# A one-core encoder layer: sums of the queries' squares from rounded high and low parts, and another lag in the key stage

## The chip, the cores and the metric

The kernel runs on one core of one Trainium2 chip. The metric is the device time of one execution in microseconds (us), lower is better. A difference of about 0.2% is what a measurement of this kernel can tell from no change.

## What is computed

One layer of a streaming encoder, for 1024 prompt tokens and 32 sample tokens (T = 1056 in all), width 1024, everything in fp32. The part that the change touches is the normalisation of queries and keys per head, before the attention:

```
xn = rms_norm(x, attn_norm)
z = xn @ w_in
q, k, v, xl, yg, gl = jnp.split(z, IN_SPLITS, axis=-1)
q = partial_rope(rms_norm(q.reshape(B, T, N_HEADS, HEAD_DIM), q_norm), positions)
k = partial_rope(rms_norm(k.reshape(B, T, N_KV_HEADS, HEAD_DIM), k_norm), positions)
...
y = x32 * lax.rsqrt(jnp.mean(x32 * x32, axis=-1, keepdims=True) + RMS_EPS)     # rms_norm
```

There are 16 query heads and 4 key heads of 64. A query sees the keys of its own chunk of 64 tokens and the chunk before. Around it stand an RG-LRU branch, output projections and a SwiGLU.

## The kernel before

Features lie on the 128 partitions, tokens in the free dimension. A dense product of this part takes one 128x1024 unit of weights and makes three blocks of 352 tokens. Each fp32 operand is split into a rounded high part and a low part (`wh`, `wl`, `acth`, `actl`, all of type f32r), and a block is 8 chunks times 3 products (high x high, high x low, low x high), so 24 matmuls. POOL makes the two parts of the next unit of weights (`split`, L522 and L524, two halves each, into a slot of two) once PE has ended the unit that was in that slot.

The program is written out by hand for each engine; the order on an engine is the order in the code, and semaphores tie the engines together. The stages that matter here are these.

- **The values**: nine products; ACT copies each from its bank to `vst` (L1054) and stores it by DMA, with two buffers. At the end ACT issues four more stores.
- **The key stage**: PE makes six blocks of keys (`qk(late, keys=True)`, 2 units x 3 blocks), then six of the first group's queries. For each block ACT runs `qk_copy`: one pass into `qsb` with the gain (L1074) and one that squares the bank. For keys the squares go into `qsq` (L1077), and PE sums them over each head with one unsplit fp32 product against `heads` (`k_sums`), which is issued two blocks late. ACT takes the root into `qstd` (`k_root`, L1087), also two copies late. DVE (`rope_k`) makes the rotation with three instructions (`halves`, L1505 to L1507), adds (L1513), takes the reciprocal of `qstd` (L1515) and multiplies (L1520).
- **The query stage**, four times, once for each group g: six blocks; ACT writes `qsb` (L1074) and the squares (L1081). The squares of group g lie in `ot[g % 2]`, the buffer which the attention of that group fills later. DVE (`rope_q`) makes `halves` and one addition into `qt` (L1525). The scale of the queries isn't multiplied in: it enters later, in the attention's `Exp`.
- **A group** (`group(g)`): PE runs four units of gate products (`dense`, 288 matmuls), and after each of them `each()` counts. After the 18th, `q_sums` issues one product for each of the 17 chunks of tokens: 128 columns of squares as the stationary operand against two columns of `heads`, unsplit fp32. After the 66th, the first attention step is issued, and one more after each 11. ACT takes the root of these sums (`q_root`, L1094), DVE the reciprocal (`q_inverse`, L1532).

The sixth block's place is the end of the query stage: on ACT and DVE its copies and its rotation run while PE is already in the first gate unit of the group.

Of the kernel before, what the change touches and what calls it, by code (L numbers as in the profile page):

```python
# [260 lines left out]
def build(nc, small_in, x_in, cs_in, w_in, kc_in, vc_in, y_out, kp_out, vp_out, ks_out, vs_out, tail_out):  # L261
# [21 lines left out]
    with ctx:  # L283
# [50 lines left out]
        with ExitStack() as s:  # L334
            cs = tensor(s, "cs", [P, 2, T])
            qsb = tensor(s, "qsb", [P, 2, BW])
            qsq = tensor(s, "qsq", [P, 2, BW])
            pt = tensor(s, "pt", [P, 2, 2 * P])
            kg = tensor(s, "kg", [P, 2, KW])
            vgr = tensor(s, "vgr", [P, AU, HD])  # L340
            qt = tensor(s, "qt", [P, 2 * T])
            tg = tensor(s, "tg", [P, 3, BW])
            pr = tensor(s, "pr", [P, 3, 2, P])
            ot = tensor(s, "ot", [P, 2, 2, T])
            snk = tensor(s, "snk", [P, 2, 2])
            sm = tensor(s, "sm", [P, 3, 6, 2])
            qroot = tensor(s, "qroot", [P, AU, 2])
            qinv = tensor(s, "qinv", [P, 2, AU, 2])
        early.close()
# [29 lines left out]

        def qsquares(g):  # L380

            return ot[:, g % 2, :, :].rearrange("p i t -> p (i t)")

# [52 lines left out]
        def flat(a):  # L436
# [21 lines left out]
            sem("rope_sin"), sem("rope_cos"), sem("rope_sum"), sem("k_rstd"), sem("rope_done"))  # L458
        heads_done, gains_loaded = sem("head_columns"), sem("gains_loaded")
        qss_done, qroot_done, qinv_done = sem("q_sumsq"), sem("q_root"), sem("q_inverse")  # L460
        k_stored = [sem(f"k_stored{i}") for i in range(2)]
# [131 lines left out]
        def _(pe):  # L593
# [131 lines left out]
            def qk(late, keys=False):  # L725

                for i in range(2):
                    for n in range(NB):
                        job = dense_block(i, n, acth, actl)
                        if keys:  # L730
                            late.append((NB * i + n, job.bank, job.after))
                        if late and (not keys or NB * i + n >= 2):
                            k_sums(*late.pop(0))
                return job

            def q_sums(g, job):

                wait(pe, free[job.bank], job.after)
                wait(pe, std_done, 6)
                wait(pe, qroot_done, 2 * g)  # L740
                wait(pe, ot_done, AU * g)
                for u in range(AU):
                    q, _, q0 = unit_shape(u)
                    i = mm(aux0[0:2 * q, 2 * u:2 * u + 2], qsquares(g)[:, 2 * q0:2 * (q0 + q)], heads[:, 0:HD:HD // 2],
                           start=True, stop=True)
                i.then_inc(qss_done, 1)
# [46 lines left out]
            def group(g, late):  # L793
                done = [0, 0]

                def each():
                    done[0] += 1
                    if done[0] == 18:
                        q_sums(g, late)
                    if done[1] < ASLOTS and done[0] == step_mm(done[1]):  # L800
# [122 lines left out]
        def _(act):  # L923
# [136 lines left out]

            act.wait_ge(unit_done, plan.units.value())
            act.wait_ge(v_stored[0], 16 * 5)
            act.wait_ge(v_stored[1], 16 * 4)
            act.wait_ge(stored, 16 * 3)
            act.wait_ge(gains_loaded, 32)


            def qk_copy(base, k, gain):
# [9 lines left out]
                else:  # L1078
                    g = base // 6 - 1
                    wait(act, ot_stored[g % 2], 16 * (g // 2))  # L1080
                    f(by_unit(qsquares(g), k % NB, k // NB), ps.rearrange("p (b t) -> p b t", t=HT), ACT.Square)\  # L1081
                        .then_inc(free[job.bank], 1)

# [5 lines left out]
            def q_root(g):  # L1089

                for j, (rows, units) in enumerate(((slice(0, P), slice(0, AU - 1)), (slice(0, 2 * DEC), slice(AU - 1, AU)))):
                    wait(act, qss_done, g + 1)
                    wait(act, qinv_done, 4 * g)
                    f(qroot[rows, units, :], aux0[rows, 2 * units.start:2 * units.stop].rearrange("p (u h) -> p u h", h=2),  # L1094
                      ACT.Sqrt, scale=1.0, bias=HD * EPS).then_inc(qroot_done, 1)
# [16 lines left out]
            qgain, kgain = gains[:, 0:1], gains[:, 1:2]  # L1112
            for j in range(12):
                qk_copy(j // 6 * 6, j % 6, (kgain, qgain)[j // 6])
                if 2 <= j < 8:
                    k_root(j - 2)
                if 3 <= j < 9:
# [213 lines left out]
        def _(dve):  # L1331
# [190 lines left out]
            def rope_q(base, k):  # L1522

                halves(base, k)
                V.tensor_tensor(by_unit(qt, k % NB, k // NB), rt1[:, :].rearrange("p (b t) -> p b t", t=HT),  # L1525
                                rt2[:, :].rearrange("p (b t) -> p b t", t=HT), ALU.add).then_inc(rope_done, 1)

            def q_inverse(g):
# [10 lines left out]
            for j in range(4):  # L1539
                rows = slice(j * HD // 2, (j + 1) * HD // 2)  # L1540
                V.memset(heads[rows, :].rearrange("p (s h n) -> p h s n", s=2, h=2)[:, j % 2], 1.0).then_inc(heads_done, 1)
            V.memset(kg[:, :, :], 0.0).then_inc(kz_done, 1)
            dve.wait_ge(cs_loaded, 32)
# [662 lines left out]
```

## Time and profile before

| | |
|---|---|
| median of three runs | 1673.92 us (1672.77 to 1674.69) |
| the profiled execution | 1678.89 us |
| its span | 1677.0 us |
| PE busy | 1620.6 us, 97% of the span |
| PE weight load busy | 1540.2 us |
| DVE, ACT, POOL busy | 1006.5, 626.0, 942.3 us |

PE is the engine that has nearly no idle time, so what counts is where PE stands still, what it issues that isn't a dense product, and which clock it is granted (TensorE has two levels, 1.2 and 2.4 GHz, given as 0.50 and 1.00). The other engines count where PE waits for them.

### The profile page before, as it was taken

How to read it: one execution, taken by the hardware profiler on the slowest of the kernel's cores; microseconds unless marked ns; L12 is line 12 of the kernel's file. 1: busy time of each engine (PE TensorE's matmuls, PEld its weight loads, DVE VectorE, ACT ScalarE, POOL GpSimd, SP SyncE). 2: the span in 40 equal slices, each digit the busy share in tenths (PEclk: the TensorE clock that was granted, in tenths of full speed). 3: DMA queues.
4: the chain of work that ended last, by engine and by line, in shares of the span. 5: the costliest groups of instructions: out<-in, count | busy, mean ns of one | idle time of the engine just before them, and what ended most of it. 6: DMA issues, size and time to landing. Idle time of an engine off the chain costs nothing. (4 is left out here: it accounts for less than half of the span.)

```text
span 1677.0 us, 28467 instructions
## 1 busy us (share of the span) xinstructions
PE 1620.6 (97%) x11270; PEld 1540.2 (92%) x11270; DVE 1006.5 (60%) x1718; ACT 626.0 (37%) x1294; POOL 942.3 (56%) x685
## 2 busy tenths in 40 slices
PE   7999998899999999999898999999999999999999
PEld 4899998889989898898897989999999999998998
DVE  6677555855545546757888878333333334869585
ACT  5535551243342525524224334333333333433232
POOL 4545542212313121468775718777677677786876
PEclk9999999999999999999999999999999999999999
DMA  5111122313132140364343512222242222373643
GB/s 183 45 51 64 63 79 84 89 56 113 47 105 67 56 128 31 101 251 165 118 154 103 180 52 79 81 83 78 77 179 78 77 77 77 141 275 117 246 143 147
DMA packets 73032, 182.09 MB, mean 109 GB/s; under 512 B 15092, under 2 KB 26676, under 8 KB 72260
## 3 DMA queue, kind: packets, MB, share of 16 engines
q1 hardware_dynamic: 52228, 160.35, 27.3%
q10 hardware_dynamic: 20672, 19.93, 3.8%
q8 instruction: 90, 1.47, 0.4%
q14 instruction: 42, 0.34, 0.1%
HBM read 131.23 MB, written 49.28 MB: 108 GB/s over the span
## 5 line engine op out<-in xcount | busy, mean ns | idle before, releaser
L597 PE MATMUL bank<-xh,wsh 128*128 128x264 f32 x2170 | 623.3, 287 | 21.8 <-POOL wsl L573 7.6
L597 PE MATMUL bank<-xh,wsl 128*128 128x264 f32 x2170 | 619.7, 286 | 0.0
L597 PE MATMUL bank<-xl,wsh 128*128 128x264 f32 x2170 | 618.8, 285 | 0.0
L597 PEld LDWEIGHTS bank<-xh,wsh 128*128 128x128 f32 x2170 | 411.3, 190 | 25.5 <-issue 16.6
L597 PEld LDWEIGHTS bank<-xl,wsh 128*128 128x128 f32 x2170 | 411.3, 190 | 0.2
L597 PEld LDWEIGHTS bank<-xh,wsl 128*128 128x128 f32 x2170 | 411.2, 190 | 0.0
L597 PE MATMUL bank<-acth,wh 128*128 128x352 f32 x960 | 318.6, 332 | 5.5 <-POOL wl L524 3.6
L597 PE MATMUL bank<-acth,wl 128*128 128x352 f32 x960 | 314.7, 328 | 0.0
L597 PE MATMUL bank<-actl,wh 128*128 128x352 f32 x960 | 313.4, 326 | 0.0
L522 POOL TENSOR_SCALAR wh<-wraw 128x512 fp32r<-128x512 f32 (+1 forms) x100 | 73.2, 732 | 404.6 <-PE bank L597 382.2
L573 POOL TENSOR_TENSOR wsl<-praw,wsh 128x512 fp32r<-128x512 f32 (+1 forms) x157 | 245.9, 1566 | 84.6 <-ACT wsh L1211 84.5
L573 POOL TENSOR_TENSOR wsl<-wsum,wsh 128x512 fp32r<-128x512 f32 (+1 forms) x120 | 185.3, 1544 | 82.5 <-ACT wsh L1211 82.4
L1211 ACT ACTIVATE wsh<-praw 128x512 fp32r<-128x512 f32 (+1 forms) x157 | 97.2, 621 | 261.7 <-PE bank L597 234.6
L597 PEld LDWEIGHTS bank<-acth,wh 128*128 128x128 f32 x960 | 183.3, 191 | 9.2 <-POOL actl L529 2.7
L597 PEld LDWEIGHTS bank<-actl,wh 128*128 128x128 f32 x960 | 183.7, 191 | 0.6
L597 PEld LDWEIGHTS bank<-acth,wl 128*128 128x128 f32 x960 | 183.0, 191 | 0.4
L1800 DVE TENSOR_TENSOR ev<-bank,ev 128x264 f32<-128x264 f32 x126 | 53.8, 431 | 158.9 <-PE bank L597 158.9
L524 POOL TENSOR_TENSOR wl<-wraw,wh 128x512 fp32r<-128x512 f32 (+1 forms) x100 | 143.4, 1434 | 8.4
L1211 ACT ACTIVATE wsh<-wsum 128x512 fp32r<-128x512 f32 (+1 forms) x120 | 74.2, 619 | 195.1 <-POOL wsum L569 120.3
L1607 DVE TENSOR_TENSOR xl<-acc,xh 128x2112 fp32r<-128x2112 f32 (+1 forms) x47 | 131.8, 2805 | 22.4 <-ACT xh L1228 22.4
L1704 DVE SCALAR_TENSOR_TENSOR ev<-bank,ev 128x264 f32<-128x264 f32 x90 | 38.7, 430 | 138.2 <-PE bank L597 137.6
L569 POOL TENSOR_TENSOR wsum<-praw,wsum 128x512 f32<-128x512 f32 (+1 forms) x45 | 71.5, 1589 | 80.7 <-PE bank L597 80.7
(179 smaller groups left out, 2305.6 us busy)
## 6 DMA issues: line engine op xcount, KB each, us to landing
praw<-in_weights SPq DMA_DIRECT2D x34, 1024.0 KB, 5.0
wraw<-in_weights SPq DMA_DIRECT2D x52, 512.0 KB, 3.3
h_scratch<-ev SPq DMA_DIRECT2D x44, 264.0 KB, 2.0
acc<-h_scratch SPq DMA_DIRECT2D x4, 2112.0 KB, 12.7
ev<-x_scratch SPq DMA_DIRECT2D x6, 1056.0 KB, 5.0
spare<-x_scratch SPq DMA_DIRECT2D x6, 1056.0 KB, 4.9
praw<-in_weights SPq DMA_DIRECT2D x8, 768.0 KB, 5.1
ta_scratch<-tg ACTq DMA_DIRECT2D x24, 176.0 KB, 1.9
```

Of the source, the lines that this page charges most:

```text
L522: nc.gpsimd.tensor_scalar(high, raw, 1.0, 0.0, ALU.mult, ALU.add).then_inc(split_done, 1)
L524: nc.gpsimd.tensor_tensor(low, raw, high.bitcast(f32), ALU.subtract).then_inc(split_done, 1)
L569: nc.gpsimd.tensor_tensor(dst, a, b, op).then_inc(wsum_done, 1)
L573: nc.gpsimd.tensor_tensor(w_slot(wsl, p, r), w_part(p, r), w_slot(wsh, p, r).bitcast(f32), ALU.subtract)\
L597: return nc.tensor.matmul(*args, **kw)
L1211: f(w_slot(wsh, p, r), w_part(p, r), ACT.Copy).then_inc(whi_done, 1)
L1607: V.tensor_tensor(xl[k][:, 0:n, :], x_part(t, k), xh[k][:, 0:n, :].bitcast(f32), ALU.subtract)\
L1704: stt(u2(par, n), bank[BANKS[2][n]][:, 0:QB], scale, u2(par, n), ALU.mult, ALU.add).then_inc(u2_done, 1)
L1800: V.tensor_tensor(dst, bank[BANKS[r][n]][:, 0:QB], (u4(par, n), None, u2(par, n), u2(par, n))[r - 3], ALU.add).then_inc(done, 1)
```

## The change

- `k_sums` and `k_root` are issued one block after the block they belong to, not two. Before the first copy of the key stage ACT no longer waits for the landing of the value stores and for the end of the value units; that wait stands before the first query copy (j == 6).
- The queries' squares are no longer summed in fp32. ACT squares the bank into `qsq`, rounds that into a high part (f32r, one more pass over `qsplit`), and DVE subtracts it from the squares to give a low part (one more pass after each `rope_q`). `q_sums` issues two accumulating f32r products for each of the 17 chunks, 34 in all, against `marks`, an f32r copy of the two columns of `heads`; the last chunk takes 128 columns too. They are issued after the 24th gate matmul instead of the 18th, and they wait for the low part of the sixth block (`qlow_done`).
- `qsplit` lies in the memory of `ot`: the high part of group g in half g % 2, the low part in the other half, which for g > 0 waits until the attention output of group g - 1 has been stored from it.

```diff
@@ tensors
+            with ExitStack() as squares:
+                qsplit = tensor(squares, "qsplit", [P, 2, 2 * T], f32r)
             ot = tensor(s, "ot", [P, 2, 2, T])
+            marks = tensor(s, "marks", [P, 2], f32r)
@@ PE
-                        if late and (not keys or NB * i + n >= 2):
+                        if len(late) > keys:
                             k_sums(*late.pop(0))
-                wait(pe, free[job.bank], job.after)
+                wait(pe, qlow_done, 6 * g + 6)
                 wait(pe, std_done, 6)
+                wait(pe, marks_done, 1)
                 wait(pe, qroot_done, 2 * g)
                 wait(pe, ot_done, AU * g)
                 for u in range(AU):
-                    q, _, q0 = unit_shape(u)
-                    i = mm(aux0[0:2 * q, 2 * u:2 * u + 2], qsquares(g)[:, 2 * q0:2 * (q0 + q)], heads[:, 0:HD:HD // 2],
-                           start=True, stop=True)
+                    c0 = min(u * P, 2 * T - P)
+                    for low in range(2):
+                        i = mm(aux0[:, 2 * u:2 * u + 2], qsquares(g, low)[:, c0:c0 + P], marks[:, :],
+                               start=low == 0, stop=low == 1)
...
-                    if done[0] == 18:
-                        q_sums(g, late)
+                    if done[0] == 24:
+                        q_sums(g)
@@ ACT
-            act.wait_ge(unit_done, plan.units.value())
-            act.wait_ge(v_stored[0], 16 * 5)
-            act.wait_ge(v_stored[1], 16 * 4)
-            act.wait_ge(stored, 16 * 3)
+            act.wait_ge(unit_done, 2 * V_PAIR)
...
-                    g = base // 6 - 1
+                    g, j = base // 6 - 1, base - 6 + k
+                    wait(act, ss_done, min(5 + j, 6))
+                    wait(act, qlow_done, j - 1)
+                    f(qsq[:, k % 2, :], ps, ACT.Square).then_inc(free[job.bank], 1)
                     wait(act, ot_stored[g % 2], 16 * (g // 2))
-                    f(by_unit(qsquares(g), k % NB, k // NB), ps.rearrange("p (b t) -> p b t", t=HT), ACT.Square)\
-                        .then_inc(free[job.bank], 1)
+                    wait(act, free[job.bank], job.after)
+                    f(by_unit(qsquares(g), k % NB, k // NB), qsq[:, k % 2, :].rearrange("p (b t) -> p b t", t=HT), ACT.Copy)\
+                        .then_inc(qhigh_done, 1)
...
             for j in range(12):
+                if j == 6:
+                    act.wait_ge(v_stored[0], 16 * 5)
+                    act.wait_ge(v_stored[1], 16 * 4)
+                    act.wait_ge(stored, 16 * 3)
                 qk_copy(j // 6 * 6, j % 6, (kgain, qgain)[j // 6])
-                if 2 <= j < 8:
-                    k_root(j - 2)
+                if 1 <= j < 7:
+                    k_root(j - 1)
@@ DVE, at the end of rope_q
+                g, j = base // 6 - 1, base - 6 + k
+                dve.wait_ge(qhigh_done, j + 1)
+                if g:
+                    dve.wait_ge(ot_stored[(g + 1) % 2], 16 * ((g + 1) // 2))
+                V.tensor_tensor(by_unit(qsquares(g, 1), k % NB, k // NB), qsq[:, k % 2, :].rearrange("p (b t) -> p b t", t=HT),
+                                by_unit(qsquares(g), k % NB, k // NB).bitcast(f32), ALU.subtract).then_inc(qlow_done, 1)
```

On ACT, at the start of the key stage (`qsb` and `qsq` of each block of keys, `qstd` its root), before:

```order
L1074 ACTIVATE qsb<-bank,gains 128x352 [waits outputs_stored,gains_loaded,v_stored1,job_done,v_stored0,unit_done]
L1077 ACTIVATE qsq<-bank 128x352
L1074 ACTIVATE qsb<-bank,gains 128x352 [waits job_done]
L1077 ACTIVATE qsq<-bank 128x352
L1074 ACTIVATE qsb<-bank,gains 128x352 [waits rope_cos,unit_done]
L1077 ACTIVATE qsq<-bank 128x352 [waits k_sumsq]
L1087 ACTIVATE qstd<-bank 128x352 [waits k_sumsq]
```

and after:

```order
L1077 ACTIVATE qsb<-bank,gains 128x352 [waits job_done,gains_loaded,unit_done]
L1080 ACTIVATE qsq<-bank 128x352
L1077 ACTIVATE qsb<-bank,gains 128x352 [waits job_done]
L1080 ACTIVATE qsq<-bank 128x352
L1094 ACTIVATE qstd<-bank 128x352 [waits k_sumsq]
L1077 ACTIVATE qsb<-bank,gains 128x352 [waits rope_cos,unit_done]
L1080 ACTIVATE qsq<-bank 128x352 [waits k_sumsq]
```

The three waits for stores have left the first row, and the root of the first block stands after the second copy instead of the third.

On DVE, two blocks of the query stage of group 0 (`rt` the rotation, `qt` its sum), before:

```order
L1505 SCALAR_TENSOR_TENSOR rt<-qsb,cs 64x352 [waits rope_done,qk_copied]
L1506 SCALAR_TENSOR_TENSOR rt<-qsb,cs 64x352
L1507 TENSOR_TENSOR rt<-qsb,cs 128x352
L1525 TENSOR_TENSOR qt<-rt 128x11x32 [waits rope_cos,rope_sin]
L1505 SCALAR_TENSOR_TENSOR rt<-qsb,cs 64x352 [waits rope_done,qk_copied]
```

and after:

```order
L1517 SCALAR_TENSOR_TENSOR rt<-qsb,cs 64x352 [waits rope_done,qk_copied]
L1518 SCALAR_TENSOR_TENSOR rt<-qsb,cs 64x352
L1519 TENSOR_TENSOR rt<-qsb,cs 128x352
L1537 TENSOR_TENSOR qt<-rt 128x11x32 [waits rope_cos,rope_sin]
L1543 TENSOR_TENSOR qsplit<-qsq,qsplit 128x11x32 [waits q_squares_high]
L1517 SCALAR_TENSOR_TENSOR rt<-qsb,cs 64x352 [waits rope_done,qk_copied]
```

A fifth instruction, with two operands in SBUF, stands between one block's rotation and the next one's.

On PE, in the first gate unit of group 0, the products that sum the queries' squares, before:

```order
L597 MATMUL bank<-acth,wl 128x352
L597 MATMUL bank<-heads,ot 128x2 [waits k_std,bank_free2]
L597 MATMUL bank<-heads,ot 128x2 x15
L597 MATMUL bank<-heads,ot 64x2
L597 MATMUL bank<-acth,wh 128x352
```

and after:

```order
L601 MATMUL bank<-acth,wl 128x352
L601 MATMUL bank<-marks,qsplit 128x2 [waits head_marks,k_std,q_squares_low]
L601 MATMUL bank<-marks,qsplit 128x2 x33
L601 MATMUL bank<-acth,wh 128x352 [waits bank_free1]
```

17 instructions become 34, and the wait for ACT's last square (`bank_free2`) becomes one for DVE's last low part.

## Rows read from the trace of the kernel before

**Rows 1.** The page's busy time: us (share of the span), instructions of each engine.

```profile
PE 1620.6 (97%) x11270; PEld 1540.2 (92%) x11270; DVE 1006.5 (60%) x1718; ACT 626.0 (37%) x1294; POOL 942.3 (56%) x685
```

**Rows 2.** Waits of PE from 255 to 342 us: engine line <- releaser: us, times, longest.

```profile
PE bank L597 <- ACT qstd L1087: 5.9, 4, 1.9
PE bank L597 <- ACT qsq L1077: 2.5, 1, 2.5
```

**Rows 3.** Timeline of ACT, start of the key stage: start us, us, instruction [idle before <-releaser].

```profile
276.53 0.55 ACT L1074 ACTIVATE qsb<-bank,gains 128x352 f32<-128x352 f32 x1 [3.26 <-DMA out_tail<-tail]
```

**Rows 4.** Timeline of DVE in the key stage, one key block and the next one's start.

```profile
284.58 0.52 DVE L1505 SCALAR_TENSOR_TENSOR rt<-qsb,cs 64x352 f32<-64x352 f32 x1
...
287.60 2.35 DVE L1515 RECIPROCAL qstd<-qstd 128x352 f32<-128x352 f32 x1 [0.76 <-ACT qstd L1087]
...
290.69 0.52 DVE L1505 SCALAR_TENSOR_TENSOR rt<-qsb,cs 64x352 f32<-64x352 f32 x1
```

**Rows 5.** Who waited for tile qstd, 270 to 320 us.

```profile
  DVE qstd L1515: 4.3, 6
  DVE rt L1505: 0.5, 1
```

**Rows 6.** Timeline of DVE and POOL, end of group 0's query stage.

```profile
322.87 0.62 POOL L522 TENSOR_SCALAR wh<-wraw 128x512 fp32r<-128x512 f32 x1 [7.49 <-PE bank L597]
...
323.89 1.51 DVE L1506 SCALAR_TENSOR_TENSOR rt<-qsb,cs 64x352 f32<-64x352 f32 x1
...
331.95 0.53 DVE L1525 TENSOR_TENSOR qt<-rt 128x352 f32<-128x352 f32 x1
```

**Rows 7.** Timeline of PE, two dense matmuls 24 apart, group 0's last query block.

```profile
318.22 0.32 PE L597 MATMUL bank<-acth,wh 128*128 128x352 f32 x1
...
322.07 0.32 PE L597 MATMUL bank<-acth,wh 128*128 128x352 f32 x1
```

**Rows 8.** Timeline of PE: the queries' sums and the first attention step, groups 0, 1, 3.

```profile
327.31 4.46 PE L597 MATMUL bank<-heads,ot 128*128 128x2 f32 x34 [1.72 <-ACT ot L1081]
...
341.98 0.38 PE L597 MATMUL bank<-kg,qt 128*128 128x128 f32 x2
423.41 0.72 PE L597 MATMUL bank<-heads,ot 128*128 128x2 f32 x6
...
438.03 0.38 PE L597 MATMUL bank<-kg,qt 128*128 128x128 f32 x2
615.53 0.39 PE L597 MATMUL bank<-heads,ot 128*128 128x2 f32 x3
...
628.61 0.38 PE L597 MATMUL bank<-kg,qt 128*128 128x128 f32 x2
```

**Rows 9.** Windows, PE: us, busy (x) of PE, PEld, DVE, ACT, POOL, granted clock, DMA.

```profile
330.40:337.30 6.90, 6.90 (x27) 6.87 (x27) 2.67 (x10) 2.00 (x4) 0.00 (x0) 0.51 0.75 130
426.00:432.80 6.80, 6.80 (x28) 6.77 (x28) 1.54 (x7) 1.99 (x4) 0.39 (x1) 0.50 0.21 77
620.60:624.00 3.40, 3.40 (x14) 3.40 (x13) 0.00 (x0) 0.81 (x2) 0.00 (x0) 0.50 0.81 274
```

**Rows 10.** Windows of the sums' products alone: PE, PEld, DVE, granted clock, DMA.

```profile
423.40:426.00 2.60, 2.59 (x24) 2.60 (x25) 0.00 (x0) 1.00 0.00 0
426.10:427.70 1.60, 1.60 (x9) 1.60 (x8) 0.00 (x0) 0.50 0.17 31
```

**Rows 11.** Timeline of DVE at group 1's and group 3's sums.

```profile
419.69 2.35 DVE L1641 TENSOR_TENSOR acc<-acc 128x2112 f32<-128x2112 f32 x1
...
425.37 1.40 DVE L1525 TENSOR_TENSOR qt<-rt 128x352 f32<-128x352 f32 x1
...
616.48 1.40 DVE L1525 TENSOR_TENSOR qt<-rt 128x352 f32<-128x352 f32 x1
```

**Rows 12.** Weight loads, mean ns: groups by line, f32r (acth) and fp32 (heads, qsq).

```profile
L597 PEld LDWEIGHTS bank<-acth,wl 128*128 128x128 f32 x960 | 183.0, 191 | 0.4
...
L597 PEld LDWEIGHTS bank<-qsq,heads x12: 186/187/190, 277.5 to 306.5; 128*128 128x128 f32 x12
```

More of the change, by code:

```diff
@@ L378, in build, with qsquares @@
         fifth = spare[:, :].rearrange("p (c t) -> p c t", t=HALF)
-        def qsquares(g):
-            return ot[:, g % 2, :, :].rearrange("p i t -> p (i t)")
+        def qsquares(g, low=0):
+            return qsplit[:, (g + low) % 2, :]
         def by_unit(a, n, i):
@@ L459, in build @@
         heads_done, gains_loaded = sem("head_columns"), sem("gains_loaded")
+        marks_done, qhigh_done, qlow_done = sem("head_marks"), sem("q_squares_high"), sem("q_squares_low")
         qss_done, qroot_done, qinv_done = sem("q_sumsq"), sem("q_root"), sem("q_inverse")
@@ L731, in qk, with q_sums @@
                             late.append((NB * i + n, job.bank, job.after))
-                        if late and (not keys or NB * i + n >= 2):
+                        if len(late) > keys:
                             k_sums(*late.pop(0))
                 return job
-            def q_sums(g, job):
-                wait(pe, free[job.bank], job.after)
+            def q_sums(g):
+                wait(pe, qlow_done, 6 * g + 6)
                 wait(pe, std_done, 6)
+                wait(pe, marks_done, 1)
                 wait(pe, qroot_done, 2 * g)
@@ L1089, in q_root @@
             def q_root(g):
-                for j, (rows, units) in enumerate(((slice(0, P), slice(0, AU - 1)), (slice(0, 2 * DEC), slice(AU - 1, AU)))):
+                for rows, bank_rows, units in ((slice(0, P), slice(0, P), slice(0, AU - 1)),
+                                               (slice(0, 2 * DEC), slice(P - 2 * DEC, P), slice(AU - 1, AU))):
                     wait(act, qss_done, g + 1)
                     wait(act, qinv_done, 4 * g)
-                    f(qroot[rows, units, :], aux0[rows, 2 * units.start:2 * units.stop].rearrange("p (u h) -> p u h", h=2),
+                    f(qroot[rows, units, :], aux0[bank_rows, 2 * units.start:2 * units.stop].rearrange("p (u h) -> p u h", h=2),
                       ACT.Sqrt, scale=1.0, bias=HD * EPS).then_inc(qroot_done, 1)
@@ L1541, in _ @@
                 V.memset(heads[rows, :].rearrange("p (s h n) -> p h s n", s=2, h=2)[:, j % 2], 1.0).then_inc(heads_done, 1)
+            dve.wait_ge(heads_done, 5)
+            V.tensor_copy(marks[:, :], heads[:, 0:HD:HD // 2]).then_inc(marks_done, 1)
             V.memset(kg[:, :, :], 0.0).then_inc(kz_done, 1)
```

## The prediction

> **What bounds the kernel now.** I read the busy time first, then the waits of PE, then the timeline of each engine around the one product that the change replaces, and the granted clock there.
>
> PE is busy for 97% of the span [rows 1]. Every time that PE stands still or runs at half clock is therefore time of the kernel, unless it stood still there anyhow; what DVE and ACT do costs only where PE waits for it. Two places matter.
>
> In the key stage PE waits for ACT's copies and roots, 5.9 and 2.5 us, 8.4 in all [rows 2]. ACT in turn waits for DVE, which is the slow engine there: a key block takes it 290.69 - 284.58 = 6.1 us, of which 0.76 is a wait for the root [rows 4], 4.3 us over six blocks, and 0.5 us more behind the last [rows 5]. A block of PE takes 322.07 - 318.22 = 3.85 us, so 0.16 us a matmul [rows 7]. So DVE leaves the key stage with a backlog: it ends the sixth query block of group 0 at 332.5 us [rows 6], while PE started the queries' sums at 327.3 [rows 8]. Before, that backlog cost PE only 1.72 us, since the sums needed ACT's squares and nothing of DVE.
>
> At the queries' sums themselves PE makes products of two columns. Their records (two for each of the 17 fp32 products) come 2.60 / 24 = 0.11 us apart, and at half clock 1.60 / 9 = about 0.2 [rows 10], so 3.8 us for all. Behind them the clock falls to 0.50 for 6.8 us in group 0 and 1 and for 3.4 in group 3 [rows 9]; group 2 is like group 1. The whole price per group is read from the distance between the first of these products and the first attention step: 48 dense matmuls are 7.7 us of it, the rest is sums and lost clock. Group 0: 14.67 - 7.7 = 7.0. Group 1: 14.62 - 7.7 = 6.9; group 2 the same. Group 3: 13.08 - 7.7 = 5.4 [rows 8].
>
> **The change part by part.**
>
> The products. 34 f32r products take the place of 34 fp32 records. No row shows an f32r product over two columns, but what sets the pace of the old ones is the load of 128 stationary columns, and such a load has the same length in both types, 191 ns for f32r and 187 for fp32 [rows 12]. I take 0.11 us each, so 3.8 us as before; the last chunk's 128 columns for 64 add 0.1. Bounds: half of it (1.9 us), if a load in f32r is shorter than its record lets one see, and twice (7.6 us), if each instruction makes two records as an fp32 one does. The Trainium skill speaks against my value: its page "TensorE: Matmul & The Clock Gate", section "Weight-path perf modes — Fast Weight Load (FWL) and DoubleRow", says that a load of 128 columns in a type other than FP32 takes a faster path, about twice as fast as measured on trn2. If f32r counts as such a type, each group saves about 1.9 us by that rule; the equal records of [rows 12] speak against it.
>
> The key stage. Two things make DVE earlier. The first copy no longer waits for stores: before, it came 3.26 us after the work ahead of it [rows 3], most of that DMA issue on ACT's own queue up to 275.2, so the gain is 276.5 - 275.2 = 1.3 us. And the root comes before DVE asks for it, since sum and root each stand a block earlier: the 4.3 + 0.5 us of waits go [rows 5]. PE now waits longer for the first sum (after two blocks, not three) but hardly afterwards, and I walk it to the end of the query blocks at 319, some 3 us earlier than 322. That gain is spent at once, as follows.
>
> The low parts. DVE gets 24 more instructions of two SBUF operands, like L1525, which take 0.53 us [rows 6] plus 0.1 between instructions; ACT gets 24 more passes of about 0.5 us, beside PE's 3.85 us a block, which hide. In group 0 nothing hides DVE's: it works through its backlog without a pause. Its end moves from 332.5 by -1.3 - 4.8 + 6 x 0.63 to 330.2. But a two-operand instruction of DVE slows while POOL splits a weight unit, 1.51 us for 0.52 [rows 6]. Such a split follows each of PE's units, four times in this stage, for 4.4 us each; before, most fell on reciprocals or on waits. With the waits gone I count 3 us more, so 333.4, between 330.2 (the collisions of before) and 335.
>
> Group 0. PE comes to the new sums at 319 + 24 x 0.16 = 322.9 and waits until 333.4, ten us. After such a wait I expect half clock: 34 x 0.215 = 7.3 us, to 340.7 (a little under twice the pace at full clock, and near the 0.2 of [rows 10]). Then the remaining 42 dense matmuls (6.7 us), with 2.6 us lost as the clock stays at half for about the 5 us that it did before. First attention step at 350.0 for 341.98 [rows 8]: **+8.0**. Bounds: DVE's end at 330.2 and full clock in the sums gives +1.3; 335 gives +9.6.
>
> Groups 1 to 3. Here DVE keeps up (four instructions and the fifth are 3 us a block, for 3.85), but the last block counts. In group 3 its rotation collides with the split and ends at 616.48 + 1.40 = 617.9 [rows 11]; the low part follows until 618.5. PE reached the old place at 615.53 and the new one, six matmuls later, at 616.5. So it waits 2.1 us where it waited for nothing. Group 2 is the same. In group 1 a 2.35 us sum for a later stage stands ahead of the sixth block on DVE, whose rotation ends at 426.8 [rows 11]; with the low parts of the fifth and sixth block I get 428.0, PE is there at 424.4, and waits 3.6 us. The idle time lies directly before 3.8 us of products of two columns, which already pull the clock down, so part of these now runs at half clock (0.1 us more for each of 34, at most 3.5) and the fall can last another stretch (3.4 us, so 1.7 lost). Bounds for the clock: 0 and 5.2 us a group. I take 2.5 in group 1, 1.5 in group 2, and 3 in group 3, which had only the short fall before. **+6.1, +3.6, +5.1**.
>
> Edits that cost nothing by cover: `marks` (one copy on DVE, before the keys arrive), the later issue of the sums (42 dense matmuls, 6.7 us, still cover ACT's root and DVE's inverse, some 2.5 us; without this cover PE would wait for them at the first step), the wait for the stored attention output (issued at 398.7 in group 1, landed some 5 us later, and the first low part is due at 404.6; a landing 3 us later would show on DVE, which has 0.8 us a block to make up for it).
>
> Sum: 8.0 + 6.1 + 3.6 + 5.1 = 22.8 us on the profiled span of 1677.0; everything behind group 3's sums is bound by PE and moves along. The profiled execution took 1678.9, 5 us over the median of the runs shown, and the difference of the two kernels should not hang on that. So 1673.9 + 22 = **1696 us**. With all lower bounds (1.3 + 3.6 + 2.1 + 2.1) it is 1683, with all upper ones (9.6 + 8.8 + 7.3 + 7.3) 1707.
>
> **The rivals.**
>
> *The clock takes no notice.* The waits cost their own time and nothing more. For it: in group 3 the sums alone cost only one short stretch. Against: every stretch of these products is followed by half clock [rows 9]. Time: 4.7 in group 0, 7.8 in the others, 1686.
>
> *The f32r products are short.* 1.9 us a group instead of 3.8, 3.6 for 7.3 at half clock. For it: each makes one pass of its moving side. Against: rows 12. That alone saves 3.7 + 3 x 2 or so: 1682 to 1687.
>
> *The f32r products are short and keep the clock up, the one that ends on the other side.* Place: the sums of each group. Price: after the wait, 1.9 us and no fall, in place of 6.9, 6.9 and 5.4: group 1 3.6 + 1.9 - 6.9 = -1.4, group 2 -2.9, group 3 -1.4, group 0 still some +3. Sum -2.7, 1671. It decides the sign from the point at which wait and products together take less than the 6.9 us of before. Against it: what pulls the clock down seems to be products of two columns, and they stay.
>
> *Each f32r product makes two records.* 3.8 us more in each of four groups, up to twice that at half clock: 1711 to 1720. For it: fp32 does so; against: f32r products over 256 and 352 columns make one.
>
> *The change doesn't do what it says*: the low part of the last block might land before PE comes there. In groups 2 and 3 that needs DVE 2 us earlier, while the split that slows it starts with the same event as the block. I see no way, 2%.
>
> **How the numbers follow.** Forecast with its own bounds (slower, 1687 to 1705): 0.62. Clock takes no notice: 0.12. Short products: 0.10. Short and clock up: 0.07, split between faster and same. Two records: 0.07. Last one: 0.02, same. The range of 8 in 10 takes in the forecast, the first two rivals and the upper bound: 1680 to 1706. Within 0.2% is 1670.6 to 1677.3, about what a measurement of this kernel can tell from no change; faster 0.04, same 0.06, slower 0.90.
>
> **What would show it.** In the profile after: no wait of DVE for `qstd`; the sums of group 0 starting at 331 to 335, with PE idle for about ten us ahead of them, ended by DVE's `qsplit`; 34 records at about 0.11 us (0.21 where the clock is 0.50); idle times of 3.6, 2.1 and 2.1 us in groups 1 to 3; first attention steps at about 350, 452, 552 and 651. Fewer or longer records than these, or a clock of 1.00 behind the sums, would move the sum as in the rivals. An idle time of under 5 us in group 0 would mean that my count of DVE's chain is wrong.

## The result, and the profile after

| | before | after |
|---|---|---|
| median | 1674.26 us (1672.77 to 1674.69, 4 runs) | 1693.62 us (1692.02 to 1696.4, 4 runs) |
| ratio | 1 | 1.0113, 95% interval 1.0101 to 1.0125 |
| the profiled execution, its span | 1678.89, 1677.0 us | 1692.57, 1690.8 us |

The change makes the kernel 1.1% slower, 19.4 us by the medians. The forecast was 1696 us. The profiled execution of before isn't one of its four runs and lies 4.6 us above their median, so the two profiles are only 13.7 us apart.

The waits of PE, from 255 to 350 us (group 0) and from 350 to 660 us (the other three), in the kernel after; they answer to [rows 2]:

```profile
PE bank L601 <- DVE qsplit L1543: 7.1, 1, 7.1
PE bank L601 <- ACT qsq L1085: 1.6, 1, 1.6
PE bank L601 <- ACT qsq L1080: 1.4, 1, 1.4
...
PE bank L601 <- DVE qsplit L1543: 6.7, 3, 3.2
PE bank L601 <- DVE ot L1606: 1.2, 3, 0.4
```

The waits for `qstd` have gone. In their place PE waits for the low parts that DVE makes: 7.1 us in group 0 and 6.7 in the three other groups. PE's timeline, the sums and the first attention steps, answers to [rows 8]:

```profile
327.62 0.59 PE L601 MATMUL bank<-marks,qsplit 128*128 128x2 f32 x2 [7.09 <-DVE qsplit L1543]
...
327.86 7.18 PE L601 MATMUL bank<-marks,qsplit 128*128 128x2 f32 x33
343.09 0.38 PE L601 MATMUL bank<-kg,qt 128*128 128x128 f32 x2
...
428.83 0.38 PE L601 MATMUL bank<-marks,qsplit 128*128 128x2 f32 x2 [3.19 <-DVE qsplit L1543]
...
444.20 0.27 PE L601 MATMUL bank<-kg,qt 128*128 128x128 f32 x1
...
628.17 0.38 PE L601 MATMUL bank<-marks,qsplit 128*128 128x2 f32 x2 [1.73 <-DVE qsplit L1543]
...
641.93 0.27 PE L601 MATMUL bank<-kg,qt 128*128 128x128 f32 x1
```

The sixth block's last instructions on DVE in group 3 (to be read beside [rows 11]) show why 1.73 us are waited there: a split of POOL runs from 622.8 to 627.3, the rotation's last instruction takes 1.41 us beside it instead of 0.53, and the low part stands behind it.

```profile
626.27 1.41 DVE L1537 TENSOR_TENSOR qt<-rt 128x352 f32<-128x352 f32 x1
627.60 0.51 DVE L1543 TENSOR_TENSOR qsplit<-qsq,qsplit 128x352 fp32r<-128x352 f32 x1
```

And the windows at half clock (us, busy (x) of PE, PEld, DVE, ACT, POOL, granted clock, DMA share, GB/s), which answer to [rows 9]:

```profile
324.30:338.00 13.70, 10.38 (x45) 10.38 (x46) 3.84 (x13) 2.11 (x4) 0.00 (x0) 0.50 0.34 73
430.10:440.30 10.20, 10.20 (x43) 10.20 (x43) 0.61 (x4) 2.11 (x4) 0.00 (x0) 0.50 0.05 20
529.10:539.30 10.20, 10.20 (x44) 10.20 (x45) 0.61 (x4) 2.11 (x4) 0.00 (x0) 0.50 0.11 43
631.50:638.30 6.80, 6.80 (x26) 6.80 (x26) 0.61 (x4) 2.11 (x4) 0.00 (x0) 0.50 0.28 99
```

Each stretch is 3.4 or 6.9 us longer than before: 41.0 us at half clock between 300 and 700 us for 23.9 (6.8 + 6.8 + 6.8 + 3.4); in group 0, PE stands still for 3.3 us of its stretch. From one group's first step to the next, after takes 101.1, 99.7 and 98.0 us, where before took 96.1, 96.1 and 94.5 (its group 2 steps at 534.11 us, the others are in [rows 8]). That is 12.2 us for the groups 1 to 3, of which 6.7 are idle time and the rest goes with the clock. Behind the last of these steps the two profiles are alike: 1690.8 - 641.93 = 1048.9 us and 1677.0 - 628.61 = 1048.4. Only group 0 looks nearly unchanged, 343.1 for 342.0. The experiments explain that.

### The profile page after: what moved, and what is told of

Same layout as the page of the kernel before. It is cut to its first block and busy times, and to the rows that moved or that the text cites. A ratio compares the mean times of both kernels' runs of the same rounds, so it can differ in the third digit from the quotient of the medians.

```text
span 1690.8 us, 28567 instructions
## 1 busy us (share of the span) xinstructions
PE 1629.9 (96%) x11270; PEld 1550.2 (92%) x11270; DVE 1019.7 (60%) x1743; ACT 638.7 (38%) x1318; POOL 947.2 (56%) x685
## 3 DMA queue, kind: packets, MB, share of 16 engines
q1 hardware_dynamic: 52228, 160.35, 27.3%
## 5 line engine op out<-in xcount | busy, mean ns | idle before, releaser
L601 PE MATMUL bank<-acth,wl 128*128 128x352 f32 x960 | 315.2, 328 | 0.0
L577 POOL TENSOR_TENSOR wsl<-praw,wsh 128x512 fp32r<-128x512 f32 (+1 forms) x157 | 254.2, 1619 | 84.6 <-ACT wsh L1223 84.6
```

The costliest lines, as they stand in the source:

```text
L577: nc.gpsimd.tensor_tensor(w_slot(wsl, p, r), w_part(p, r), w_slot(wsh, p, r).bitcast(f32), ALU.subtract)\
L601: return nc.tensor.matmul(*args, **kw)
```

## The experiments

My theory: after is slower because DVE's low parts make PE wait, and the wait lengthens the stretch at half clock; the key stage alone gains. Rivals: f32r products over two columns are dearer (or cheaper) than fp32 ones; the key stage counts for nothing; the clock has nothing to do with the wait. Each group of runs was compared with before on its own chip, whose median was 1675.6 to 1676.9 us, so the ratios are to be compared and not the times. The last column is read from one profiled execution of each kernel.

| kernel | ratio to before, 95% interval | at half clock between 300 and 700 us |
|---|---|---|
| after, once more | 1.0091 (1.0070 to 1.0111) | 41.0 |
| key stage alone | 0.9972 (0.9959 to 0.9984) | 23.9 |
| split sums alone | 1.0126 (1.0113 to 1.0140) | 44.4 |
| after, sums behind the 48th matmul | 1.0005 (0.9992 to 1.0019) | 27.3 |
| after, group 0's sums behind the 60th | 1.0066 (1.0045 to 1.0088) | 30.7 |
| after, high products alone | 1.0015 (1.0003 to 1.0027) | 23.9 |
| after, no low parts | 0.9951 (0.9937 to 0.9965) | 20.5 |
| key stage, fp32 sums behind the 48th | 0.9941 (0.9918 to 0.9964) | 20.5 |
| before, sums spread | 0.9970 (0.9951 to 0.9988) | 20.5 |
| key stage, sums spread | 0.9961 (0.9946 to 0.9976) | 17.1 |
| key stage, sums spread where nothing waits | 0.9904 (0.9888 to 0.9919) | 0.0 |

### Before once more

> The kernel before once more, for a second profile of the same program. In the first profile of before the copies of the key stage began at 276.5 us, in the one of after at 271.6, although only some 1.3 us of that can be the change. Theory: the landing of the value stores differs from execution to execution, so a second profile shows the first key copy somewhere else, by up to 4 us, and the first attention step of group 0 with it. Rival: the start is fixed at 276.5 and the change moved it by 5 us.

Its profiled execution took 1676.22 us. Timeline of ACT at the start of the key stage:

```profile
271.18 0.46 ACTq L1059 DMA_DIRECT2D out_tail<-tail  x1
274.43 0.56 ACT L1074 ACTIVATE qsb<-bank,gains 128x352 f32<-128x352 f32 x1 [4.77 <-DMA out_tail<-tail]
```

The first copy comes at 274.4, not at 276.5 [rows 3]; the copies of `vst` ahead of it wait for landings, and those differ. So the theory holds, and the rival falls: of the 5 us between the two first profiles some 2 are the execution's own. What the prediction didn't have: in this execution the last store was issued at 271.2 and the copy still had to wait for landings that take up to 4 us, so taking the waits away gives 2.9 us here, not 1.3. In the executions with the new key stage the first copy began at 270.6 to 272.2 us, in the four with the old one at 274.4 to 276.5. The first step of group 0 stands at 339.7 here, so after's 343.1 is 3.4 us late against this profile and 1.1 against the first.

### The two parts of the change alone

```diff
-            act.wait_ge(unit_done, plan.units.value())
-            act.wait_ge(v_stored[0], 16 * 5)
...
-                        if late and (not keys or NB * i + n >= 2):
+                        if len(late) > keys:
...
-                if 2 <= j < 8:
-                    k_root(j - 2)
+                if 1 <= j < 7:
+                    k_root(j - 1)
```

> Before with the key stage of after (sums and roots a block earlier, stores waited for later), the queries' sums untouched. Theory: DVE's waits for the roots go (4.8 us in the profile of before) and the first copy comes 1.3 us or more earlier, which lets PE end the query blocks of group 0 earlier: 2 to 5 us faster, 1670 to 1672, nothing changed in groups 1 to 3. Rival: PE's longer wait for the first sum takes it all back, no change at 1674. In the first case the split sums alone cost more than the whole change does.

0.9972: 4.7 us faster, at the upper end of what was expected. PE waits in the stage:

```profile
PE bank L597 <- ACT ot L1078: 2.6, 1, 2.6
PE bank L597 <- ACT qsq L1074: 1.2, 1, 1.2
PE bank L597 <- POOL wh L522: 0.9, 1, 0.9
```

The 5.9 us of waits for `qstd` [rows 2] have gone. 0.9 us of waits for POOL are new: PE comes so early that the next unit's split isn't ready.

The second half, after with these edits undone:

> After with the key stage of before. Theory: the low parts' work comes on top of the whole backlog of DVE: idle time before group 0's sums of about 10 us instead of 7.1 + 1.6, and 3.2, 1.7, 1.7 us in groups 1 to 3 as in after: 1697 to 1700. Rival: the key stage counts for nothing in either kernel, then 1694 as after.

1.0126, 21 us slower than before and 1696.9 in its own chip's times. The theory's sign is right, the size at its lower end (1697 to 1700). The idle time ahead of group 0's sums didn't grow to 10 us: PE's waits for `qstd` came back, 6.4 us, and beside them stand the same 7.0 us for the low part.

```profile
PE bank L601 <- DVE qsplit L1542: 7.0, 1, 7.0
PE bank L601 <- ACT qstd L1097: 6.4, 4, 2.0
```

That follows from the chains: the old key stage makes DVE late and PE late as well, by about the same amount. The parts add up within their intervals: -0.28% and +1.26% make +0.98% beside the +1.13% and +0.91% of the two comparisons of after.

### The wait taken away by covering it

```diff
-                    if done[0] == 24:
+                    if done[0] == 48:
                         q_sums(g)
```

> After with the queries' sums issued after the 48th gate matmul instead of the 24th, 3.85 us of dense work later. Theory (PE waits for the last low part, and the wait lengthens the stretch at half clock): the idle times of groups 1 to 3 (3.2, 1.7, 1.7) go, group 0's 7.1 falls to 3.3, so 10.5 us less idle time, and 4 to 6 us less lost to the clock: 1678 to 1682. Rival (the products themselves or their number cost the time, the wait is beside it): 1690 or more, with the stretches of half clock as long as in after.

1.0005: the loss against before has gone, with all low parts made and all 34 products issued. That is 0.9 to 1.1% under after, 14 to 18 us, where the theory had 14 to 17. A part of this is the gain of the key stage, which this kernel has as well: against the key stage alone (0.9972) 0.3% are still lost. The waits of PE from 255 to 660 us:

```profile
PE bank L601 <- DVE qsplit L1543: 3.3, 1, 3.3
PE bank L601 <- DVE ot L1606: 1.6, 4, 0.4
```

The three waits of groups 1 to 3 have gone, group 0's has fallen by the 3.85 us of dense work. In groups 1 to 3 the stretches at half clock are 6.8, 6.8 and 0 us. So the rival that puts the time into the products falls. Group 0, where 3.3 us of the wait are left, keeps its long stretch:

```profile
327.80:341.50 13.70, 13.46 (x56) 13.46 (x57) 0.98 (x8) 2.47 (x5) 0.00 (x0) 0.50 0.20 40
```

```diff
-                    if done[0] == 24:
+                    if done[0] == (24 if g else 60):
```

> After with the sums of group 0 alone issued after the 60th gate matmul; those of groups 1 to 3 stay after the 24th. Theory: group 0's idle time falls from 7.1 to about 1.3 us and the clock isn't low when its sums start: 6 to 9 us below after, of the 17 that the move of all four groups to the 48th brought; groups 1 to 3 keep their idle times of 3.2, 1.7 and 1.7 us and their stretches at half clock. Rival (the groups 1 to 3 hold nearly all): 3 us or less.

1.0066, so 4 us under after on the same chip (1.0091) and 8 under the first comparison; 6 to 9 were expected, and with so wide an interval the times alone don't decide between this and the rival. By the profile group 0's first step comes at 334.9 us, 8.2 before after's, and groups 1 to 3 keep their three waits:

```profile
PE bank L601 <- DVE qsplit L1543: 8.0, 4, 3.2
```

The stretches at half clock, in the order of the groups:

```profile
328.70:338.90 10.20, 10.20 (x41) 10.15 (x42) 1.95 (x9) 3.80 (x11) 1.40 (x2) 0.50 0.11 37
424.20:431.00 6.80, 6.80 (x30) 6.80 (x30) 0.61 (x4) 2.11 (x4) 0.00 (x0) 0.50 0.01 2
523.20:530.00 6.80, 6.80 (x28) 6.80 (x28) 0.61 (x4) 2.11 (x4) 0.00 (x0) 0.50 0.00 0
622.20:629.00 6.80, 6.80 (x26) 6.80 (x26) 0.61 (x4) 2.11 (x4) 0.00 (x0) 0.50 0.25 90
```

Here the expectation was wrong: with the same waits of 3.2, 1.7 and 1.7 us, groups 1 and 2 have 6.8 us at half clock and not 10.2, as much as in the first profile of before, where nothing is waited for. So the wait does not lengthen the stretch by the same amount in every execution. Over groups 1 to 3 the stretches add up to 20.4 us here, to 27.3 in both profiles of after and to 30.7 in the kernel with the split sums alone, against 17.1 in both profiles of before: longer each time, by 3 to 14 us.

Against the key stage alone, whose first step is at 335.96 us and which takes 286.6 us from there to group 3's, after loses 7.1 us in group 0 and 12.3 in the other three. This kernel has nothing of the first loss and 11.0 us of the second. By the profiles group 0 thus holds some four tenths of what the split sums cost.

### What the products cost

```diff
-                    for low in range(2):
-                        i = mm(aux0[:, 2 * u:2 * u + 2], qsquares(g, low)[:, c0:c0 + P], marks[:, :],
-                               start=low == 0, stop=low == 1)
+                    i = mm(aux0[:, 2 * u:2 * u + 2], qsquares(g)[:, c0:c0 + P], marks[:, :], start=True, stop=True)
```

> After with only the 17 products of the high parts: the low part is still made by DVE and waited for, but left out of the sums. Theory: the idle times stay (7.1, 3.2, 1.7, 1.7) and each missing product saves 0.11 us at full and 0.21 us at half clock, so 1.9 to 3.6 us a group, 8 to 14 in all, with some stretches of half clock shorter: 8 to 16 us below after. Rival (a second product into the same sums costs nearly nothing, or the time is all in the wait): within 3 us of after.

1.0015, 13 to 16 us under after, the upper end of the theory, while PE's waits for `qsplit` are the same 13.7 us:

```profile
426.16 2.06 PE L601 MATMUL bank<-marks,qsplit 128*128 128x2 f32 x17 [3.20 <-DVE qsplit L1541]
...
PE bank L601 <- DVE qsplit L1541: 13.7, 4, 7.0
```

The 17 products take 2.06 us and the next matmul begins 1.92 us after their start, so 0.11 each. More than half of the gain is the clock: 23.9 us at half clock for 41.0. In this kernel the waits are there and the stretches add up to what they do in before. So the wait alone doesn't lengthen them; the next kernel shows the same of a row of 34 products without a wait.

```diff
-                wait(pe, qlow_done, 6 * g + 6)
+                wait(pe, qhigh_done, 6 * g + 6)
...
-                        i = mm(aux0[:, 2 * u:2 * u + 2], qsquares(g, low)[:, c0:c0 + P], marks[:, :],
+                        i = mm(aux0[:, 2 * u:2 * u + 2], qsquares(g)[:, c0:c0 + P], marks[:, :],
...
-                V.tensor_tensor(by_unit(qsquares(g, 1), k % NB, k // NB), qsq[:, k % 2, :].rearrange("p (b t) -> p b t", t=HT),
-                                by_unit(qsquares(g), k % NB, k // NB).bitcast(f32), ALU.subtract).then_inc(qlow_done, 1)
```

> After without the low parts: DVE's 24 subtractions are left out, PE waits for ACT's high part alone and makes both products of each chunk from it, so 34 f32r products stay. Theory: 34 f32r products cost what 34 fp32 records did, and only the wait for DVE made after slow: no idle time before the sums but one of group 0, and the time of the key stage alone (0.2 to 0.4% under before, 1668 to 1673 where before is 1676). Rival (f32r products over two columns are dear, or pull the clock down for longer): above before by 4 us or more.

This kernel adds the high part twice, so its sums are too large and only its time is of use. 0.9951, 1667.9 us on a chip where before is 1675.6: 0.5% under before, where the theory had 0.2 to 0.4. 34 f32r products, in groups 0 and 1:

```profile
320.18 3.96 PE L601 MATMUL bank<-marks,qsplit 128*128 128x2 f32 x34 [0.41 <-ACT qsplit L1088]
...
414.75 3.85 PE L601 MATMUL bank<-marks,qsplit 128*128 128x2 f32 x34
```

3.85 us for 34 is 0.113 each, which is what an fp32 record took [rows 10]. This settles the price of the products: neither the short load nor the double record. It also isolates the low parts: with them after stands 1.4 to 1.6% above this kernel, 23 to 27 us, of which the idle time ahead of the sums is 13.7 - 0.4 us; the rest goes with 20 us more at half clock, where about half of each us is lost. With the row of 34 products and hardly a wait, 20.5 us stand at half clock: fewer than in before. It takes the wait and the long row together to get the 41.0 of after.

### The row of products, and the clock

In both kernels the sums stand in one row of products of two columns, and the clock falls in or behind each. I took the row apart, with the unsplit sums of before:

```diff
-                    if done[0] == 18:
-                        q_sums(g, late)
+                    if 18 <= done[0] < 18 + 2 * AU and done[0] % 2 == 0:
+                        q_sums(g, late, (done[0] - 18) // 2)
```

> The key stage of after and the unsplit fp32 sums of before, but the 17 products of a group issued singly, one after each second gate matmul from the 18th to the 50th. Theory (the row of products of two columns is what takes the clock down): between dense matmuls they leave the clock at 1.00, so the 6.8 us stretches behind the sums go and with them 2.5 to 3.5 us a group, 10 to 14 us in all against the key stage alone: 0.8 to 1.2% under before. Rival one: the clock falls all the same, nothing gained. Rival two: each product between dense ones costs more than 0.22 us since a dense load is no longer hidden, and the gain is halved or gone.

> Before with the sums spread in the same way and nothing else changed. Theory: 10 to 14 us under before, the same step as from the key stage alone to the key stage with spread sums. If the two steps differ by more than 3 us, the gain hangs on what stands ahead of the sums in group 0.

0.9961 and 0.9970: 0.1 and 0.3% gained where 0.6 to 0.8 was expected. The two steps are 1.8 and 5.0 us, about the 3 us apart that the second text allows, and their intervals are too wide to tell them from equal; both are small. The granted clock of the first of these kernels tells why, in windows of groups 0, 1 and 2:

```profile
322.00:339.10 17.10, 17.10 (x67) 16.70 (x67) 3.35 (x11) 2.35 (x5) 0.00 (x0) 0.50 0.28 57
421.50:430.70 9.20, 9.20 (x69) 8.97 (x67) 3.47 (x5) 0.00 (x0) 2.99 (x3) 1.00 0.15 57
514.70:523.80 9.10, 9.10 (x68) 8.87 (x67) 2.39 (x4) 0.00 (x0) 1.89 (x2) 1.00 0.17 58
```

In groups 1 to 3 the clock never falls: from step to step they take 93.1 us, for 94.5 to 96.1 with the row. A product between two dense matmuls costs (9.1 - 32 x 0.16) / 17 = 0.23 us, what its two records cost in the row, so rival two falls. But in group 0 the spread sums start right after an idle time:

```profile
320.57 0.38 PE L597 MATMUL bank<-heads,ot 128*128 128x2 f32 x2 [2.64 <-ACT ot L1079]
```

The clock was still at 1.00 when the first of them began; it falls at 322.0 and stays at 0.50 for 17.1 us, until 3 us after the last spread product (336.2). The second kernel's profile has the same in group 0, after an idle time of 1.7 us:

```profile
325.54 0.38 PE L597 MATMUL bank<-heads,ot 128*128 128x2 f32 x2 [1.74 <-ACT ot L1082]
...
327.40:344.50 17.10, 17.10 (x68) 16.70 (x67) 3.69 (x12) 2.35 (x5) 0.00 (x0) 0.50 0.38 78
```

In the first kernel that costs group 0 4.2 us against the key stage alone (first step at 340.15 for 335.96), of the 7.2 that the other groups gained.

The medians hide something that the single executions show. Of ten executions of the second kernel, six took 1672.3 to 1675.3 us at a mean granted clock of 0.987 to 0.991, and four took 1661.7 to 1668.1 at 0.995 to 0.997; of nine of the first kernel, two took 1662.6 and 1664.3 us at 0.993 to 0.994, the others 1669.7 to 1673.2 at 0.988 to 0.991. Both profiles are of the slower kind. So some executions of the second kernel were 8 to 14 us under before, about what the theory had (10 to 14). It is likely that they did without the long stretch in group 0; none of them was profiled, so that is not shown.

The last kernel moves only group 0's start:

```diff
+                    first = 18 if g else 34
-                    if 18 <= done[0] < 18 + 2 * AU and done[0] % 2 == 0:
-                        q_sums(g, late, (done[0] - 18) // 2)
+                    if first <= done[0] < first + 2 * AU and done[0] % 2 == 0:
+                        q_sums(g, late, (done[0] - first) // 2)
```

> Key stage of after, unsplit fp32 sums spread singly over every second gate matmul as in the run before, but in group 0 from the 34th matmul (to the 66th) instead of the 18th. Theory: in group 0 the spread sums were entered after an idle time of 2.6 us, the clock had fallen to 0.50, and at that clock the mixed stretch was too thin to raise it again: 17.1 us at half clock. Entered without a wait, the clock stays at 1.00 in group 0 too: no stretch of half clock between 300 and 700 us, first attention step at 331 to 333 instead of 340, 7 to 9 us below the spread run, about 1662 to 1665 where before is 1676 (0.7 to 0.9% under before). Rival: the fall comes from the mixed stretch itself, and group 0 stays where it was.

0.9904, 1660.5 us where before is 1676.9: faster than both kernels, and a little more than expected. All five executions lie between 1659.8 and 1663.0 us. Windows of groups 0 and 1, and the first step of group 0:

```profile
322.00:340.00 18.00, 17.59 (x118) 16.38 (x119) 8.78 (x32) 6.41 (x23) 3.81 (x4) 1.00 0.46 118
418.00:431.00 13.00, 13.00 (x86) 12.58 (x86) 4.65 (x16) 4.83 (x17) 3.91 (x4) 1.00 0.12 37
...
330.33 0.49 PE L597 MATMUL bank<-kg,qt 128*128 128x128 f32 x2
```

The same mixed stretch, entered without a wait ahead of it, keeps the full clock: 330.3 instead of 340.15. The rival, that the mixed stretch itself brings the fall, is out. That the stretch was "too thin" to bring the clock back is the expectation's own reading; no run shows a reason, and in that profile the clock fell 1.4 us after the stretch had begun, not ahead of it.

The control for it, one row of fp32 sums, only later:

> Key stage of after, unsplit fp32 sums in one row as in before, but after the 48th gate matmul. Theory: only group 0 had an idle time ahead of the sums (2.65 us), so at most 2.7 us and perhaps one short stretch of half clock are gained against the key stage alone: 1666 to 1671; the falls behind the row of sums stay in all groups. Rival (late sums are better in themselves): 1662 or less.

0.9941: group 0's idle time has gone and 3.4 us at half clock with it, the rows' falls stay (20.5 us). Its interval reaches to 0.9964, so against the key stage alone (0.9972) it gains 1 to 9 us; the profiles differ by 3 us, as the theory has it. By its median of 1667.9 us being late is not what makes the spread version fast. Two of its seven executions (1660.2 and 1662.8 us, mean clock 0.994) were as fast as the spread version, though; what differed in them no profile shows.

This kernel is also the one to hold the split sums behind the 48th matmul (1.0005) against: the same key stage and the same place, with fp32 squares. Split sums still cost 0.6% there, and the profiles put it into group 0, whose first step comes at 331.9 us here and at 340.7 there. Covering the wait made up for the loss, but not for all that the low parts cost.

> The changed kernel once more, beside the others on one chip: 1.0101 to 1.0125 times before, as in the first comparison, with idle times ahead of the sums of 7.1, 3.2, 1.7 and 1.7 us within 0.5 us. If the idle times differ from these, they hang on the execution and not on the program.

1.0091: the expectation is missed by 0.1%, though the intervals overlap. The idle times ahead of the sums are 6.8, 3.2, 1.7 and 1.7 us, so they belong to the program, and the 41.0 us at half clock are there again. In the key stage this execution differs (a stretch of 3.4 us at half clock at 273.5 us, which the first had not), and it still comes to group 0's first step at 343.6, within half a us of the first: what sets this end is DVE.

## Why the prediction was right, and where its steps were off

**The sign, the place and the mechanism** were right: PE waits for the low part of the sixth block, ended by `qsplit`, in all four groups, and the wait lengthens the stretch at half clock. Covering the wait takes the loss against before away. The forecast of 1696 is 2.4 us off, closer than its terms are, and that is in part luck, as follows.

**The products: 0.11 us each.** Right, 0.113 without a wait ahead, and (334.90 - 327.62) / 34 = 0.214 at half clock. The Trainium skill ("TensorE: Matmul & The Clock Gate", section "Weight-path perf modes — Fast Weight Load (FWL) and DoubleRow") has loads of 128 columns about twice as fast when the type isn't FP32; if f32r counted as such a type, they would have taken about half, and the 0.113 of these runs doesn't show that. The rivals with short products and with two records are out.

**The key stage: forecast -1.3 and -4.8 us for DVE.** The waits for `qstd` went, as said. The first copy gained 2.9 us and not 1.3: the step that failed is that I read the whole price of the wait for the stores from one execution, in which the stores were issued late and landed in 1.5 us. In others they are issued earlier and land in 3 to 4 us.

**DVE's end in group 0: 333.4, measured 327.6.** Three sizes. The start was 272.2 instead of 275.9 us, so 3.7. A whole query block with its low part took 2.72 us instead of 3.0 (without it 2.36), since the low part begins while the addition ahead of it still runs, so 1.7 in six. A key block was 5.24 instead of 5.35, so 0.7. Timeline of DVE, key block to key block and query block to query block:

```profile
285.24 0.52 DVE L1517 SCALAR_TENSOR_TENSOR rt<-qsb,cs 64x352 f32<-64x352 f32 x1
...
290.48 0.52 DVE L1517 SCALAR_TENSOR_TENSOR rt<-qsb,cs 64x352 f32<-64x352 f32 x1
...
311.25 0.52 DVE L1517 SCALAR_TENSOR_TENSOR rt<-qsb,cs 64x352 f32<-64x352 f32 x1
...
313.97 0.52 DVE L1517 SCALAR_TENSOR_TENSOR rt<-qsb,cs 64x352 f32<-64x352 f32 x1
```

The collisions with POOL's splits were sized well: the chain from 272.2 to 327.6 is 55.4 us, undisturbed it would be 6 x 5.24 + 6 x 2.72 = 47.8, so they cost 7.6; the forecast had 3 us more than in before, whose chain lost about 4.5.

**Group 0: +8.0, measured +1.1 against the first profile of before and +3.4 against the second.** PE waited 7.1 us, not ten: DVE ended 5.8 us earlier, and PE was there at 320.5 instead of 322.9. The sums did run at half clock, for 7.3 us, but only 3.1 us of half clock were left behind them and not 5. PE's 1.6 us ahead of the last query block are ACT's, which was issuing the stores of the keys until 315.2; since DVE's end sets the start of the sums, they cost nothing more. The sums started outside the 331 to 335 us that the prediction gave as its sign. The time of this group is the term that was most oversized.

**Groups 1 to 3: +6.1, +3.6, +5.1, measured +5.1, +3.6, +3.5.** Idle times 3.2, 1.7 and 1.7 for 3.6, 2.1 and 2.1; the stretches at half clock are 3.4 us longer in each, as forecast, and what goes beyond the idle time is 1.9, 1.9 and 1.8 us for 2.5, 1.5 and 3.

**The sum, +22.8, measured in the profiles +13.3 to group 3's first step** (641.93 - 628.61) and 13.7 at the end. Of the 9.5 us too many, 6.9 are group 0's and 2.6 the others'; no term came out larger than forecast. By the medians the change costs 19.4 us, 5.7 more than by the profiles: 4.6 since the profiled execution of before lay above its median, 1.1 since that of after lay below. The forecast put an oversized sum on the median, and the medians happen to lie further apart than the profiles: that is the luck in it. Against the second profile of before, 1676.22 us, the profiled execution of after is 16.4 slower. What the executions at the median do otherwise than the profiled ones stays open. Three slips of arithmetic are without effect: 330.2 + 3 is 333.2 and not 333.4, 1673.9 + 22.8 is 1696.7, and twice the price in the rival of two records would reach 1726 and not 1720.

**The rival with the unchanged clock** (1686) fell: the stretches did lengthen in all groups of both profiles of after. By its time alone, 12.5 us, it would have fitted the 13.3 of the profiles better than the forecast; the granted clock decides. One thing was missing in the forecast and in the rivals: that the fall behind the row of sums is itself a price which can be avoided, some 11 us together with the wait that precedes it (0.9904 for 0.9972).

## What to carry to other kernels

Where PE bounds a kernel, price a new wait together with what stands behind it: a short idle time directly ahead of a row of tiny products cost 1.6 to 2.1 times its own length in after, since the clock stayed low for longer. Putting such products singly between large ones, and beginning only where nothing had to be waited for, gave the fastest kernel here. And count a chain on an engine that has a backlog from its start in more than one execution; what begins it can hang on the landing of a DMA.

## What the runs showed of the hardware that I had not expected

- The same mix of products (two dense ones of 352 columns, one fp32 one of two columns) ran at 1.00 in all ten profiled groups in which nothing was waited for ahead of it, and went to 0.50 for 17.1 us in both in which PE had just stood still, for 2.6 and 1.7 us. By their times, some executions of the same two kernels escaped this.
- In every group of both profiles of before, 3.4 or 6.8 us at half clock began in the row of 34 short records or shortly behind it, although PE was busy there throughout (2.59 of 2.60 us in [rows 10]).
- Two-operand instructions of DVE that overlap a split of POOL took up to 1.51 us for 0.52, and a chain of DVE lost 7.6 us to four splits of 4.5 us, as both engines ran all the time.
- A store of 128 KB of the values landed in 1.7 us or in up to 4.1 within one execution, and the first one of its stage in 7.4 to 9.7 us.
